# Three quarters of a token turn moved into the product before it, in a two-block transformer kernel on one core

## The reference, cut to what matters

```python
h = h + dsa_mixer(rms_norm_2(h, a_attn_norm), ..., a_w_o, ...)            # ends in  out @ w_o
h = h + sq_relu_mlp(rms_norm_2(h, mlp_norm[0]), mlp_w_up[0], mlp_w_down[0])
# layer 1
ckr = rms_norm_2(h, kv_norm) @ w_dkv          # c_kv, k_rope
q   = rms_norm_2(rms_norm_2(h, b_attn_norm) @ w_dq, q_lora_gain) @ w_uq
kv  = rms_norm_2(ckr[..., :256], kv_lora_gain) @ w_ukv
h = h + mla_mixer(...)                        # ends in  out @ w_o
h = h + sq_relu_mlp(rms_norm_2(h, mlp_norm[1]), mlp_w_up[1], mlp_w_down[1])

def sq_relu_mlp(h, w_up, w_down):
    return jnp.square(jax.nn.relu(h @ w_up)) @ w_down
```

## Time and profile before

| | us |
|---|---|
| median of 3 runs | 1739.24 (1739.08 to 1740.36) |
| time of the profiled execution | 1742.56 |
| its span | 1740.8 |
| TensorE busy in matmuls | 1392.6 (80%) |
| VectorE / ScalarE busy | 533.4 (31%) / 389.7 (22%) |
| mean granted clock of TensorE | 0.878 of full |

### The profile page before, as it was taken

One profiled execution on the slowest core, in us unless ns is written; L12 is line 12 of the kernel. 1 busy time (PEld: TensorE's weight loads), 2 busy tenths in 40 slices (PEclk: granted clock), 3 DMA queues, 4 the chain that ended last, 5 costly groups with the idle time before them and its releaser, 6 DMA issues.

```text
span 1740.8 us, 20823 instructions
## 1 busy us (share of the span) xinstructions
PE 1392.6 (80%) x8546; PEld 844.0 (48%) x8546; DVE 533.4 (31%) x893; ACT 389.7 (22%) x580; POOL 137.1 (8%) x102
## 2 busy tenths in 40 slices
PE   4999987676667666666775666598999999899999
PEld 1886432222122112212221222176899988889997
DVE  2595320000000000000000000068365557636554
ACT  3415200000000000000000000067433355643332
POOL 1620000000000000000000000024300000720000
PEclk8999978878787887887778887799999999799999
DMA  9677589999999999999999999972255544225552
GB/s 374 238 290 306 211 327 428 428 428 428 429 429 428 429 429 428 428 428 429 428 428 429 428 428 428 424 257 98 97 193 184 178 157 154 76 97 193 182 181 97
DMA packets 79682, 542.00 MB, mean 311 GB/s; under 512 B 6186, under 2 KB 9595, under 8 KB 51858
## 3 DMA queue, kind: packets, MB, share of 16 engines
q1 hardware_dynamic: 76320, 535.93, 75.5%
q0 software_dynamic: 1584, 5.03, 0.9%
q10 hardware_dynamic: 1730, 0.36, 0.1%
HBM read 540.22 MB, written 1.08 MB: 311 GB/s over the span
## 4 chain that ended last, share of the span: by engine, by line
DMA 47%; PE 44%; DVE 3%; issue 2%; ACT 1%; POOL 1%; ACTq 1%; SPq 0%; DVEq 0%; POOLq 0%
DMA ring<-in_w_down 23%; DMA ring<-in_w_up 23%; PE bank L1304 10%; PE bank L1306 10%; PE bank L1305 10%; PE bank L1639 3%; PE bank L1656 3%; PE bank L1532 2%; DMA ring<-in_w_in 1%; PE bank L1334 1%; PE bank L1513 1%; PE bank L1453 1%; PE bank L1900 1%; PE bank L1505 1%; POOL big_parts L708 1%
## 5 line engine op out<-in xcount | busy, mean ns | idle before, releaser
L1639 PE MATMUL bank<-ring,low 128*32 128x512 f32 x2016 | 321.6, 784 | 163.1 <-DMA ring<-in_w_up 135.0
L1639 PEld LDWEIGHTS bank<-ring,low 128*32 128x32 f32 x2016 | 67.5, 133 | 401.7 <-DMA ring<-in_w_up 208.0
L1656 PE MATMUL bank<-ring,low 128*32 128x512 f32 x992 | 170.5, 822 | 101.1 <-DMA ring<-in_w_down 93.4
L1060 ACT ACTIVATE low<-bank 128x512 f32<-128x512 f32 x16 | 9.6, 597 | 848.9 <-PE bank L1639 848.9
L865 ACT ACTIVATE ring_parts<-ring 128x4096 fp32r<-128x4096 f32 (+3 forms) x46 | 151.9, 3301 | 204.3 <-DMA ring<-in_mlp_w_down 93.6
L1957 DVE TENSOR_TENSOR ring_parts<-ring,ring_parts 128x4096 fp32r<-128x4096 f32 (+2 forms) x35 | 148.4, 4244 | 143.6 <-ACT ring_parts L865 143.6
L1306 PE MATMUL bank<-feat_parts,ring_parts 128*128 128x256 f32 x640 | 181.9, 284 | 0.0
L1305 PE MATMUL bank<-feat_parts,ring_parts 128*128 128x256 f32 x640 | 181.9, 284 | 0.0
L1304 PE MATMUL bank<-feat_parts,ring_parts 128*128 128x256 f32 x608 | 173.9, 286 | 6.5 <-DVE feat_parts L2027 3.9
L2304 DVE TENSOR_TENSOR low<-low,bank 128x512 f32<-128x512 f32 x16 | 11.0, 687 | 475.3 <-PE bank L1639 475.3
L1656 PEld LDWEIGHTS bank<-ring,low 128*32 128x32 f32 x992 | 31.6, 130 | 223.0 <-DMA ring<-in_w_down 160.9
(11 more groups left out here) (392 smaller groups left out, 1948.6 us busy)
## 6 DMA issues: line engine op xcount, KB each, us to landing
ring<-in_w_gate SPq DMA_DIRECT2D x64, 2048.0 KB, 25.9
ring<-in_w_up SPq DMA_DIRECT2D x62, 2048.0 KB, 23.0
ring<-in_w_down SPq DMA_DIRECT2D x62, 2048.0 KB, 26.3
ring<-in_mlp_w_up SPq DMA_DIRECT2D x16, 2048.0 KB, 8.1
ring<-in_mlp_w_down SPq DMA_DIRECT2D x16, 2048.0 KB, 7.8
ring<-in_w_mod SPq DMA_DIRECT2D x12, 2048.0 KB, 16.3
ring<-in_w_in SPq DMA_DIRECT2D x3, 2048.0 KB, 11.6
ring<-in_a_w_in SPq DMA_DIRECT2D x3, 2048.0 KB, 18.0
```

What stands on the lines that cost most here:

```text
L1639: last = pe.matmul((GATE if i < 4 else UP)[32 * j:32 * j + 32, :], xsT[:, k, :], held(n, 2)[:, kk, 512 * j:512 * j + 512], start=(k == 0), ...
L1656: last = pe.matmul(TURN[32 * g:32 * g + 32, :], hidT[:, c, 32 * j:32 * j + 32], down_row(n, c)[:, 512 * d:512 * d + 512], start=(j == 0 an ...
```

## The change

It does three things, the first at all three hand-overs.

- Twelve of the sixteen transposes (`turn_early`: tile 0 whole, tile 1's first half) are issued inside the last group of the product before: behind 12 of 24 matmuls of `ao11` and `bo11`, and behind 6 of 12 of group (1,1) of `down(7)`. The last four (`turn_half(.., 1, 1)`) come later: in `up(0)` behind the first half of the contraction (k = 0 to 3) of tiles m = 0 and m = 2, after which the second halves of these tiles follow, then the tiles 1 and 3 whole; in the second hand-over behind k = 0 to 3 of `ckr0`, after which `ckr1` does k = 0 to 3, and then both do k = 4 to 7.
- DVE makes the low parts of banks 0 and 1 before its last addition, those of 2 and 3 after it.
- ACT does `weights_high(dq_c)` ahead of `rms` of tile 0, and DVE does `gained_low(dq_c)` for k = 0 to 2 between the additions (0,1) and (1,0) of `down(7)`, and for k = 3, 4 between (1,0) and (1,1).

```diff
@@ ACT
             warm_root()
+            weights_high(dq_c, gain=V_B)
             rms("rb", x, xn, D, lambda t: [(sem("xm0"), 2 * (t + 1))], [0])
-            weights_high(dq_c, gain=V_B)
             parts_high("bT", hb)
@@ TensorE
+            def turn_half(name, t, d, ready):
+                pe.wait_ge(*ready(t, d))
+                for i in (2 * d, 2 * d + 1):
+                    if t == 0:
+                        banks.wait_free(pe, f"{name}{i}")
+                    for k in (2 * i, 2 * i + 1):
+                        c = (k % 2) * T + t * P
+                        last = pe.transpose(bk(f"{name}{i}")[:, c:c + P], x[:, t, k * P:(k + 1) * P], ident)
+                    if t == NT - 1:
+                        end(last, f"{name}{i}")
+
+            def turn_early(name, ready):
+                for t, d in ((0, 0), (0, 1), (1, 0)):
+                    turn_half(name, t, d, ready)
...
-                        token_major_split(f"{names}{t}{n}", hT, split_as(c, KD, 512), t * P, 512)
+                        last_one = (t, n) == (NT - 1, 1)
+                        token_major_split(f"{names}{t}{n}", hT, split_as(c, KD, 512), t * P, 512,
+                                          ready=(lambda k: turn_early(turned, lambda t, d: drained(f"{names}{t}{d}")) if k == 4 else None)
+                                          if last_one else None)
...
+                    else:
+                        for half in range(2):
+                            relu_done(half)
+                            banks.wait_all_free(pe, f"mlp{layer}", [half])
+                            tile(2 * half, range(0, KD // 2))
+                        turn_half(f"m{layer}T", NT - 1, 1, lambda t, d: drained(f"{'ab'[layer]}o{t}{d}"))
+                        for half in range(2):
+                            tile(2 * half, range(KD // 2, KD))
+                        tile(1, range(KD)).then_inc(sem("ml_up"), 1)
+                        last = tile(3, range(KD))
                     used(last)
...
                             for kk in range(4):
+                                if layer == 0 and c == N_FC - 1 and (t, d, kk) == (1, 1, 2):
+                                    turn_early("bT", after_mlp)
...
+            need_split(dkv_c)
+            for k0 in (0, KD // 2):
+                for t in range(NT):
+                    if k0 == 0:
+                        banks.wait_free(pe, f"ckr{t}")
+                    for k in range(k0, k0 + KD // 2):
+                        if t == 0 and k % 2 == 0:
+                            pe.wait_ge(*drained(f"bT{k // 2}"))
+                        last = split_product(...)
+                    if k0:
+                        end(last, f"ckr{t}")
+                    elif t == 0:
+                        turn_half("bT", NT - 1, 1, after_mlp)
@@ VectorE
+                        if (t, n) == (NT - 1, 1):
+                            parts_low(f"m{layer}T", hA2, v=V_MLP + KD * layer, pairs=[0, 1])
                         dve.wait_ge(*banks.filled(f"{name}{t}{n}"))
...
                         else:
                             dve.wait_ge(chunk_used, mlp_chunk(layer, N_FC - 1, True) + 1)
+                        if layer == 0 and (t, d) == (1, 1):
+                            parts_low("bT", hb, pairs=[0, 1])
                         xs = x[:, t, 512 * d:512 * d + 512]
                         dve.scalar_tensor_tensor(out=xs, in0=SUM[2 * t + d][:, :], scalar=r2[:, t:t + 1], in1=xs,
                                                  op0=ALU.mult, op1=ALU.add).then_inc(sem(done), 1)
-                if layer == 0:
-                    gained_low(dq_c, V_B, range(0, 3))
+                        if layer == 0 and (t, d) == (0, 1):
+                            gained_low(dq_c, V_B, range(0, 3))
+                        if layer == 0 and (t, d) == (1, 0):
+                            gained_low(dq_c, V_B, range(3, 5))
```

More of the change, by code:

```diff
@@ L1772, in _, with out_product @@
             attend_pairs("sa", sa_scores, sa_values, pa, reverse, sa_between)
-            def out_product(names, cs, hT, pre):
+            def out_product(names, cs, hT, pre, turned):
                 for t in range(NT):
@@ L1779, in out_product @@
                         need_split(c)
-                        token_major_split(f"{names}{t}{n}", hT, split_as(c, KD, 512), t * P, 512)
-            out_product("ao", wo2, hA2, "sa")
+                        last_one = (t, n) == (NT - 1, 1)
+                        token_major_split(f"{names}{t}{n}", hT, split_as(c, KD, 512), t * P, 512,
+                                          ready=(lambda k: turn_early(turned, lambda t, d: drained(f"{names}{t}{d}")) if k == 4 else None)
+                                          if last_one else None)
+            out_product("ao", wo2, hA2, "sa", "m0T")
             def mlp(layer):
@@ L1791, in up, with tile @@
                     need_split(n, turn_n)
[L1792 to L1796, removed]
+                    def tile(m, ks):
+                        for k in ks:
                             if c == 0 and m == 0 and k % 2 == 0:
@@ L1801, in up, with relu_done @@
                                                  [h[:, k, :] for h in hA2], k == 0, k == KD - 1)
-                        if m == 1:
-                            last.then_inc(sem("ml_up"), 1)
+                        return last
+                    def relu_done(half):
+                        if n0 + 2 * c + half > 1:
+                            pe.wait_ge(sem("ml_relu"), n0 + 2 * c + half - 1 + turn)
+                    if c:
+                        for m in range(4):
+                            if m % 2 == 0:
+                                relu_done(m // 2)
+                            last = tile(m, range(KD))
+                            if m == 1:
+                                last.then_inc(sem("ml_up"), 1)
+                    else:
[8 more added lines that the diff above has]
+                        last = tile(3, range(KD))
                     used(last)
@@ L1818, in down @@
                     used(last)
-                banks.wait_all_free(pe, f"mlp{layer}", range(2))
                 up(0)
@@ L1829, in mlp, with after_mlp @@
                 down(N_FC - 1)
-            turn_tokens(x, "m0T", half_ready=lambda t, d: drained(f"ao{t}{d}"))
+            def after_mlp(t, d):
+                return sem("xm0"), 2 * t + d + 1
             mlp(0)
-            turn_tokens(x, "bT", half_ready=lambda t, d: (sem("xm0"), 2 * t + d + 1))
             def turn_latents(name, k0, nk, src):
@@ L1851, in keys_values @@
                                       t * P, 512)
-            down_product(dkv_c, "ckr", KV_LORA + QK_ROPE, 0, "bT")
-            down_product(dkv_c, "ckr", KV_LORA + QK_ROPE, 1)
+            need_split(dkv_c)
[6 more added lines that the diff above has]
+                            pe.wait_ge(*drained(f"bT{k // 2}"))
+                        last = split_product(bk(f"ckr{t}")[:, 0:KV_LORA + QK_ROPE], [h[:, k, t * P:(t + 1) * P] for h in hb],
+                                             [w[:, k, :] for w in split_as(dkv_c, KD, KV_LORA + QK_ROPE)], k == 0, k == KD - 1)
+                    if k0:
+                        end(last, f"ckr{t}")
+                    elif t == 0:
+                        turn_half("bT", NT - 1, 1, after_mlp)
             down_product(dq_c, "dq", Q_LORA, 0)
@@ L1907, in _ @@
             attend_pairs("la", la_scores, la_values, bo, ident, la_between)
-            out_product("bo", wo3, boT, "la")
-            turn_tokens(x, "m1T", half_ready=lambda t, d: drained(f"bo{t}{d}"))
+            out_product("bo", wo3, boT, "la", "m1T")
             mlp(1)
@@ L2453, in _, with residual @@
             attend_pairs("sa", sa_bias, pa, hA2, sa_between)
-            def residual(name):
+            def residual(name, layer):
                 for t in range(NT):
                     for n in range(2):
+                        if (t, n) == (NT - 1, 1):
+                            parts_low(f"m{layer}T", hA2, v=V_MLP + KD * layer, pairs=[0, 1])
                         dve.wait_ge(*banks.filled(f"{name}{t}{n}"))
@@ L2474, in mlp @@
             def mlp(layer, done):
-                parts_low(f"m{layer}T", hA2, v=V_MLP + KD * layer)
+                parts_low(f"m{layer}T", hA2, v=V_MLP + KD * layer, pairs=[2, 3])
                 def units(c, blocks=0):
@@ L2517, in mlp @@
                                                  op0=ALU.mult, op1=ALU.add).then_inc(sem(done), 1)
-                if layer == 0:
-                    gained_low(dq_c, V_B, range(0, 3))
-            residual("ao")
+                        if layer == 0 and (t, d) == (0, 1):
+                            gained_low(dq_c, V_B, range(0, 3))
+                        if layer == 0 and (t, d) == (1, 0):
+                            gained_low(dq_c, V_B, range(3, 5))
+            residual("ao", 0)
             mlp(0, "xm0")
-            parts_low("bT", hb)
-            gained_low(dq_c, V_B, range(3, KD))
```

(4 more changed lines are left out.)

## The result

The changed kernel is **slower by 0.37%** (ratio 1.0037, 95% interval 1.0027 to 1.0048). The medians are 1750.03 us for the changed kernel (11 runs, 1744.73 to 1753.05) and, with more runs than stood ahead of the prediction, 1741.23 us for the one before (11 runs, 1738.60 to 1744.55). The forecast of 1746.2 stood against a median of 1739.24, a ratio of 1.0040. Taken as a time, 1750.03 lies 0.7 us above the stated range, and the kernel before lies 2.0 us above its first three runs.

The account below looks back on a forecast made before the run. It took TensorE's standstills between products to be what the change could win. Hand-overs of 0.35, 0.35 and 4.45 plus 1.8 for the clock gave +6.95 us, 1739.24 to 1746.2 us; range 1743.2 to 1749.3.

Parts of the forecast that it names:

- First and third hand-over, +0.35 each: Around the start of `up(0)` in both MLPs: the stall becomes 1.86 us where it was 1.44, taken as +0.35 us each.
- the late turn is followed by its own consumer: In `up(0)`: nothing stands between the last four transposes and the matmul needing their parts, so TensorE stalls 1.86 us.
- DVE stands in `gained_low`: Second hand-over: DVE waits about 4.6 us for ACT's high part of `w_dq`, ahead of the addition of (1,0).
- TensorE stands in `down(7)` for 3.15 us: Inside the last group of `down(7)`: the third turn half waits for DVE's addition of (1,0), a stall of 3.15 us.
- The end of `down(7)` sets the time, through the load of `w_ukv`: Second hand-over: `down(7)` ends 4.45 us late, and the load of `w_ukv` and the chain behind it move as much.
- The clock falls, +1.8: Behind the stall in `down(7)`: TensorE's clock halves and the ten instructions left take twice their time, +1.8 us (0 to 1.8).
- The twelve transposes in `down(7)`, +1.31: Inside the last group of `down(7)`: twelve transposes account for 1.31 us of its 4.45 us late end.
- The stretches of 1.86 us dropping the clock: Rival, in `up(0)` at first and third hand-over: these stalls halve the clock too, +2 us each, 1750.2 us; chance 0.07.
- `w_dq` in time: Rival, second hand-over: `w_dq`'s high part is ready, no stall in `down(7)`, +2.0 us in all, 1741.2 us; chance 0.11.
- The slice with the low clock: Profile's second block: one slice near 1440 us was read as the exception to TensorE being busy at full clock.
- the 28th slice: Start of the second block's MLPs: from here on TensorE was read as busy nine tenths and more at full clock.
- The upper end of the range: Whole kernel: 1749.3 us, the forecast with 0.6 for 0.35 twice and one fall of the clock in an `up(0)`.

Follow-up runs that it names:

- e4: Only the first and third hand-over changed, the second as in the kernel before; ratio 1.0008 to the kernel before.
- e5: e4 with the late half turn between the two half tiles of `up(0)` instead of behind both; ratio 0.9988 to the kernel before.
- e1: Changed kernel with DVE's `gained_low(dq_c)` pieces moved behind all additions of `down(7)`; ratio 1.0012 to the kernel before.
- e2: Changed kernel with `gained_low(dq_c)` for k = 0 to 4 behind the addition of (1,0), none ahead of it; ratio 1.0006 to the kernel before.
- e7: Kernel before with ACT's and DVE's work on `ckr` ahead of the parts of `w_ukv` instead of behind them; ratio 0.9993 to the kernel before.
- e3: Only the second hand-over changed, the first and third as in the kernel before; ratio 1.0025 to the kernel before.
- e10: Changed kernel with one `gained_low(dq_c)` piece instead of three between the additions (0,1) and (1,0); ratio 1.0022 to the kernel before.
- e11: e5 and e7 together, with DVE's work on the first tile of `dq` also ahead of its part of `w_ukv`; ratio 0.9978 to the kernel before.

## Why the prediction was right

Point by point:

- **First and third hand-over, +0.35 each.** Right: e4 has +0.36 and +0.28. The stall was taken as 1.86 us and is 1.78 in the same measure (1.62 by the brackets). The reading that the late turn is followed by its own consumer is shown by e5, where one half tile between them leaves 0.19.
- **DVE stands in `gained_low`.** Right: 4.76 us, against 4.6 forecast. Its place ahead of the addition of (1,0) is what costs (e1 and e2 against the changed kernel, 4.6 to 4.8 us).
- **TensorE stands in `down(7)` for 3.15 us.** Right: 3.14 in the same measure, 2.98 by the brackets.
- **The end of `down(7)` sets the time, through the load of `w_ukv`.** Right: the load is 6.17 us later, the turn of `ckr` 6.42 less the first hand-over's 0.36, which is 6.06. The distance of 18.3 to 18.7 us from the load to the turn in nine profiles shows it best; e2 shows that `ckr0` can start 1.0 us later for nothing, e7 that DVE's part of `w_ukv` stood before the turn.
- **The clock falls, +1.8.** In the profiled execution 1.68; in e3's, the same stall, 0.80. That the clock falls was right; that nearly all of the 1.8 arrived in the profile is in part luck, since it was taken at its upper end. The page of the Trainium skill that the prediction cites (TensorE: Matmul & The Clock Gate, "Part 1: The HAM clock gate") had said that it would vary.
- **The twelve transposes in `down(7)`, +1.31.** Right: with the stall gone 1.79 - 0.36 = 1.43 is left (e1).
- **The stretches of 1.86 us dropping the clock, or `w_dq` in time.** Neither happened: the clock was full through both waits of 1.62, and the load of `w_dq` took as long as before.

The sum, +6.95, was 0.7 us above what the profile shows and 0.0003 above the ratio; the medians differ by 8.8 us. What the working did not see is the attention: it moved by 0.5 us between the two profiles shown, and by up to 7 us among all. That both of these profiles have the long stretch at half clock is luck: one with the short stretch would have moved the sum by 1 to 5 us. Two readings in it are wrong and carried nothing in the sum. The slice with the low clock is the attention from 1480 us on, and the 28th slice is busy eight tenths. The upper end of the range, by its own words (0.25 us more at two hand-overs and 2 us for one fall of the clock), is 1748.7 and not 1749.3. The spread of the three runs before, 1.3 us, was all there was to tell how far executions of one kernel differ; with 11 runs it is 6 us.

## What to carry to other kernels

Before work is moved into another engine's product, ask what that product's end releases: here it was a DMA, and a wait that costs nothing a few instructions later cost all of its length ahead of that end. An early turn pays only if something else stands between it and its first consumer, here one half tile against a latency of 1.9 us. And an operation that waits for a load should not stand in an in-order list ahead of one that TensorE waits for.

## What the hardware showed that was not expected

The clock of TensorE fell after short idle times, and often only when TensorE was at work again: after 2.06 us, 1.2 us behind the restart (e10), after 2.47 us, 1.6 us behind it (e2, before `ckr0`), and after 2.96 us, 1.0 us behind it (e3). In the attention it fell in each of the twelve profiles, 0.2 to 3.0 us behind the end of a wait of 1.81 (e11) to 2.19 us (before) that follows 48 transposes. It stayed full through all waits of 1.28 to 1.69 us at the hand-overs. Idle time may not be the right count: in e10 3.5 us lie between two matmuls of `down(7)`, filled in part by twelve transposes. But in the kernel before 3.6 us with sixteen lie between `down(7)` and `ckr0`, and there the clock stayed full. These rows do not decide it.

And in the attention, where TensorE waits for 1.9 to 2.5 us a second time (2.52 in the kernel before, 1.93 in e2), the clock that had fallen to 1.2 GHz stayed there for 10 us in some profiles and for 20 in others of like code, worth 1 to 5 us of 1740: more than most single edits of this kernel.
